# A twentieth early weight load for the expert layer, and scatters and gathers at other places between its steps

## The reference, cut to what matters

```python
def expert_choice_ffn(x, w_router, w_gate_up, w_down):
    B, T, D = x.shape                                  # 1, 512, 1024
    cap = EC_CAPACITY_FACTOR * T // N_EXPERTS          # 64 tokens for each of 16 experts
    logits = jnp.einsum('btd,de->bte', x, w_router)
    aff = jax.nn.softmax(logits, axis=-1)
    gate, idx = lax.top_k(jnp.swapaxes(aff, 1, 2), cap)
    xs = x[bidx, idx]                                  # each expert gathers its 64 tokens
    h = jnp.einsum('becd,edf->becf', xs, w_gate_up)    # 1024 -> 2 x 1024
    hg, hu = jnp.split(h, 2, axis=-1)
    ye = jnp.einsum('becf,efd->becd', jax.nn.silu(hg) * hu, w_down)   # 1024 -> 1024
    ye = ye * gate[..., None]
    return jnp.zeros_like(x).at[bidx, idx].add(ye)     # scattered back, summed
```

## Time and profile before

| what | value |
|---|---|
| median of 3 runs | 2118.4 us (2118.39 to 2119.78) |
| the profiled execution: its time, its span | 2120.5 us, 2118.7 us |
| busy in the span: TensorE, VectorE, ScalarE, GpSimd | 98%, 48%, 35%, 7% |
| TensorE's granted clock, mean | 0.997 |
| moved by DMA | 352 MB, 166 GB/s on average |
| the expert steps, first up step to the end | 1661.7 to 2118.7 us |

### The profile page before, as it was taken

How to read it: one execution, slowest core, us unless ns; L and a number is a source line. 1 busy time by engine, 2 the same in 40 slices (tenths; PEclk the granted TensorE clock), 3 DMA queues, 4 the chain that set the end, 5 groups by cost and what they waited for, 6 DMA issues and landing times.

```text
span 2118.7 us, 24857 instructions
## 1 busy us (share of the span) xinstructions
PE 2086.6 (98%) x10137; PEld 1517.1 (72%) x10137; DVE 1023.1 (48%) x1515; ACT 750.2 (35%) x1076; POOL 146.4 (7%) x149
## 2 busy tenths in 40 slices
PE   9999999999999999999999999999999999999998
PEld 7878888888777778888888877777787544444433
DVE  7875433445666664434446656564464312122123
ACT  7774322323455543222334456533333100011012
POOL 0220000001000020000001010062101000000000
PEclk9999999999999999999999999999999999999999
DMA  6233223324211123233233322242236999999996
GB/s 218 75 104 110 83 83 124 100 69 121 70 60 59 61 92 105 69 123 99 82 88 119 115 60 77 60 89 72 73 110 231 401 426 412 427 427 426 426 427 275
DMA packets 88944, 352.09 MB, mean 166 GB/s; under 512 B 9472, under 2 KB 24064, under 8 KB 64512
## 3 DMA queue, kind: packets, MB, share of 16 engines
q1 hardware_dynamic: 83856, 342.48, 43.6%
q0 software_dynamic: 2192, 2.63, 1.0%
q10 hardware_dynamic: 2784, 5.41, 0.7%
HBM read 347.06 MB, written 2.10 MB: 165 GB/s over the span
## 4 chain that ended last, share of the span: by engine, by line
PE 86%; DVE 5%; DMA 4%; ACT 3%; issue 2%; POOL 0%; ACTq 0%; DVEq 0%; SPq 0%; POOLq 0%
PE PS L2184 20%; PE PS L2185 19%; PE PS L2186 19%; PE PS L2591 9%; PE PS L2631 4%; DMA SL<-in_wgu_dram 3%; PE PS L2227 2%; DMA SL<-in_wdn_dram 1%; DVE WL L1664 1%; PE PS L2301 1%; PE PS L2575 1%; PE PS L2325 1%; PE PS L2315 1%; PE PS L2576 1%; DVE XC L1731 1%
## 5 line engine op out<-in xcount | busy, mean ns | idle before, releaser
L2184 PE MATMUL PS<-HH,WH 128*128 128x512 f32 x1392 | 553.9, 398 | 3.0 <-DVE HL L1704 2.2
L2186 PE MATMUL PS<-HH,WL 128*128 128x512 f32 x1392 | 543.0, 390 | 0.0
L2185 PE MATMUL PS<-HL,WH 128*128 128x512 f32 x1392 | 542.6, 390 | 0.0
L1664 DVE TENSOR_TENSOR WL<-RAW,WH 128x1024 fp32r<-128x1024 f32 (+4 forms) x302 | 343.5, 1138 | 294.6 <-ACT WH L1340 293.7
L1340 ACT ACTIVATE WH<-RAW 128x1024 fp32r<-128x1024 f32 (+4 forms) x302 | 286.5, 951 | 308.5 <-PE PS L2186 278.3
L2184 PEld LDWEIGHTS PS<-HH,WH 128*128 128x128 f32 x1392 | 261.7, 188 | 69.1 <-issue 10.3
L2186 PEld LDWEIGHTS PS<-HH,WL 128*128 128x128 f32 x1392 | 261.7, 188 | 55.6
L2185 PEld LDWEIGHTS PS<-HL,WH 128*128 128x128 f32 x1392 | 262.0, 188 | 52.9 <-issue 1.0
L2591 PE MATMUL PS<-SL,XS 128*64 128x512 f32 x928 | 220.8, 595 | 6.4 <-DMA SL<-in_wgu_dram 5.8
L2591 PEld LDWEIGHTS PS<-SL,XS 128*64 128x64 f32 x928 | 70.4, 137 | 135.7 <-issue 133.7
L2186 PE MATMUL PS<-MH,WL 128*128 128x512 f32 x352 | 136.9, 389 | 0.0
(11 more groups left out here) (375 smaller groups left out, 2740.5 us busy)
## 6 DMA issues: line engine op xcount, KB each, us to landing
SL<-in_wgu_dram SPq DMA_DIRECT2D x116, 1024.0 KB, 21.8
SL<-in_wdn_dram SPq DMA_DIRECT2D x55, 1024.0 KB, 24.8
RAW<-in_w_dram SPq DMA_DIRECT2D x46, 512.0 KB, 3.4
RAW<-in_wg_dram SPq DMA_DIRECT2D x44, 512.0 KB, 3.4
RAW<-in_wu_dram SPq DMA_DIRECT2D x44, 512.0 KB, 3.4
RAW<-in_wd_dram SPq DMA_DIRECT2D x32, 384.0 KB, 3.1
RAW<-in_wqkv_dram SPq DMA_DIRECT2D x24, 512.0 KB, 3.5
RAW<-in_wd_dram SPq DMA_DIRECT2D x32, 320.0 KB, 2.9
```

The costliest lines, as they stand in the source:

```text
L1664: e.tensor_tensor(wl, raw, wh.bitcast(F), ALU.subtract).then_inc(*wlo.did("u", u))
L2184: e.matmul(out, wh[:, w], xh, start=k == 0, stop=False)
L2185: e.matmul(out, wh[:, w], xl, start=False, stop=False)
L2186: m = e.matmul(out, wl[:, w], xh, start=False, stop=k == g.total - 1)
```

## The change

It has four parts. (1) A twentieth slot, used once, for load 15: the gate half goes to the storage of GT, the two quarters of the up half to HG[0] and HG[1], by three transfers with one semaphore; the matmuls now address each slot as four pieces of 512 columns. This takes load 15's place in the ring from it, and the loads behind it move by one slot until load 41. (2) The gathers of q + 1 keep only their first two in the odd pair, behind up step 1; the other six move into the even pair, two behind up steps 1, 3 and 5, just ahead of the steps that read them, as in pair 0 before. (3) In pairs 1 to 6 the scatter moves from in front of the turns to behind the down steps: block 0 behind step 0, block 1 behind step 1, blocks 2 and 3 behind step 2. (4) In pairs 2, 4 and 6 the one-hot's transposes and the next one-hot move from behind down step 0 to behind down step 3.

```diff
--- before.py
+++ after.py
@@ -30,7 +30,7 @@
 CAP = 64
 NEARLY = 10
 NRING = 16
-SPARE = ((4, 23), (0, 39), (1, 39))
+SPARE = ((4, 23), (0, 39), (1, 39), (15, 15))
 NBACK = 4
 NGATE = 5
 NWARM = 21
@@ -843,12 +843,12 @@
             gather(0, 1)
         for k in range(8):
             o.add("up", i, k)
-            if i % 2 and i < 7 and k % 2:
-                gather(q + 1, k - 1)
-                gather(q + 1, k)
-            if i == 0 and k % 2 and k < 7:
-                gather(0, k + 1)
-                gather(0, k + 2)
+            if i % 2 and i < 7 and k == 1:
+                gather(q + 1, 0)
+                gather(q + 1, 1)
+            if i % 2 == 0 and k % 2 and k < 7:
+                gather(q, k + 1)
+                gather(q, k + 2)
             if i == 7 and 1 <= k < 5:
                 scatter(6, k - 1)
                 o.add("halves", k - 1)
@@ -864,8 +864,6 @@
             o.release(("h", i, 2 + n), "mul", i, n)
         if i == 0:
             o.add("alpha")
-        elif i < 7:
-            scatter(i - 1, *range(4))
         for half in range(2):
             o.claim("ht", i, half)
             o.add("h_turn", i, half)
@@ -884,13 +882,15 @@
             break
         for k in range(4):
             o.add("down", i, k)
-            if i % 2 == 0 and k == 0:
+            if i % 2 == 0 and k == (3 if i else 0):
                 for j in range(2):
                     o.claim("gt", "e", q, j)
                     o.add("scatter_t", q, j)
                     o.release(("gt", "e", q, j), "turn", "gt", q, j)
                 if q < 3:
                     o.add("one_hot", q + 1)
+            if 0 < i < 7 and k < 3:
+                scatter(i - 1, *((0,), (1,), (2, 3))[k])
         y_out(0)
         y_out(1)
 
@@ -1109,8 +1109,12 @@
         pa.close()
         YOH = sb("YOH", [128, D], R, px)
         YOL = sb("YOL", [128, D], R, px)
+        pa = ExitStack()
+        SG = sb("SG", [128, 2 * T], F, pa)
+        pa.close()
         GT = [sb(f"GT{i}", [128, T], R, px) for i in range(2)]
-        SL = early + late + once + x_slots
+        SL = [[t[:, 512 * n:512 * n + 512] for n in range(4)] for t in early + late + once + x_slots]
+        SL.append([SG[:, 0:512], SG[:, 512:1024], HG[0], HG[1]])
         assert CST["ones"] + 2560 == NCST and len(early) == NEARLY and len(SL) == NRING + len(SPARE)
         BN = sb("BN", [128, 4, 2, 6], F, px)
         MV = sb("MV", [128, 4, 2], F, px)
@@ -1199,6 +1203,8 @@
         ring = [i for i in range(len(SL)) if i not in where]
         where.update((i, j) for j, i in enumerate(ring))
         issue = ring[:NEARLY] + [SPARE[0][0]] + ring[NEARLY:NEARLY + 2] + [SPARE[1][0], SPARE[2][0]] + ring[NEARLY + 2:]
+        issue.append(SPARE[3][0])
+        whole = early + late + once + x_slots
         turns = [where[i] for i in range(len(SL))]
         for i in range(len(SL), len(loads)):
             while i > spare.get(turns[0], i):
@@ -1242,10 +1248,14 @@
                 if j in last_in:
                     e.wait_ge(*ex("w", last_in[j] // 2))
                 last_in[j] = i
-                if i < len(loads) - 4:
-                    e.dma_start(SL[j][:, :], src).then_inc(*d_slot[j].did(i))
+                if i == SPARE[3][0]:
+                    e.dma_start(SG[:, :], src[:, 0:1024]).then_inc(*d_slot[j].did(i, "gates"))
+                    e.dma_start(HG[0], src[:, 1024:1536]).then_inc(*d_slot[j].did(i, "first ups"))
+                    e.dma_start(HG[1], src[:, 1536:2048]).then_inc(*d_slot[j].did(i))
+                elif i < len(loads) - 4:
+                    e.dma_start(whole[j][:, :], src).then_inc(*d_slot[j].did(i))
                 else:
-                    dst = SL[j][:, :].rearrange("p (e f n) -> p e f n", e=2, f=2)
+                    dst = whole[j][:, :].rearrange("p (e f n) -> p e f n", e=2, f=2)
                     e.dma_start(dst[:, 0], src[0]).then_inc(*d_slot[j].did(i, "first"))
                     e.dma_start(dst[:, 1], src[1]).then_inc(*d_slot[j].did(i))
             for half, c in ((0, 2), (0, 0), (0, 6), (0, 4), (1, 2), (1, 6)):
@@ -2589,7 +2599,7 @@
                         for e2 in range(2):
                             x0 = (2 * (i % 2) + e2) * 64
                             m = e.matmul(bank("h", i, n)[64 * e2:64 * e2 + 64, :], XS[:, k, x0:x0 + 64],
-                                         SL[slot(l0 + e2)][:, 512 * n:512 * n + 512], start=k == 0, stop=k == 7)
+                                         SL[slot(l0 + e2)][n], start=k == 0, stop=k == 7)
                         if k == 7 and n == 2:
                             m.then_inc(*ex.did("h", i, 0))
                     m.then_inc(*ex.did("w", 12 * i + k))
@@ -2629,7 +2639,7 @@
                         for n in range(2):
                             for e2 in range(2):
                                 m = e.matmul(bank("y", i, n)[64 * e2:64 * e2 + 64, :], HT[k // 2][:, 2 * (k % 2) + f, 64 * e2:64 * e2 + 64],
-                                             SL[slot(l0 + e2)][:, 1024 * f + 512 * n:1024 * f + 512 * n + 512],
+                                             SL[slot(l0 + e2)][2 * f + n],
                                              start=k + f == 0, stop=k == 3 and f == 1)
                     m.then_inc(*ex.did("w", 12 * i + 8 + k))
                     if k == 3:
@@ -2641,9 +2651,8 @@
                     e.wait_ge(*d_slot[slot(l0)](l0))
                     for f in range(2):
                         for e2 in range(2):
-                            col = 1024 * e2 + 512 * f
                             m = e.matmul(bank("y", 7, n)[64 * e2:64 * e2 + 64, :], HT[1][:, 2 * x + f, 64 * e2:64 * e2 + 64],
-                                         SL[slot(l0)][:, col:col + 512], start=False, stop=x + f == 2)
+                                         SL[slot(l0)][2 * e2 + f], start=False, stop=x + f == 2)
                     if x:
                         m.then_inc(*ex.did("y", 7, n))
                 elif kind == "scatter":
```

## The result

The changed kernel takes 2124.0 us (median of 9 runs, 2122.7 to 2126.8), the kernel before 2118.7 beside it (9 runs, 2118.4 to 2120.7). The ratio is 1.0025 with a 95% interval of 1.0016 to 1.0033: 5.2 us slower. I had forecast 2116.2 and a range up to 2119.0. The profiled execution took 2123.2 us with a span of 2121.4; it reached its first up step 1.4 us earlier than the one of before (1660.27 against 1661.66), so of its experts the loss is 4.1 us.

The account below looks back on a forecast made before the run. The weight stream was taken as the bound: the end is load 187's landing plus 31.5 us. Early load -0.4, second gap -1.8, order on TensorE 0 give -2.2 us from 2118.4: 2116.2 us, range 2113.5 to 2119.0.

Parts of the forecast that it names:

- 0 (order on TensorE): Term of the sum for the moved gathers and scatters: TensorE's work is only reordered, costing 0 us.
- Rival (4): TensorE becomes the bound in pair 6, gather pairs holding up the next up steps: +4.3 us, 2122.7; chance 0.05.
- The early load: Load 15 in its own storage: worth 2.46 us until about 1680, 0 to 1.5 after 1705; taken as 0.4.
- 34 slots: Loads allowed before any down step ends: 34 instead of 35, so load 34 waits for down step (0,0), 1702.12.
- the first gap: Weight stream at 172 GB/s from 1663 to 1668 us, 2.98 us lost; the change was to fill 2.46.
- a new loss before 1706: New gap in the weight stream at load 34: 0.9 us on the lagging engine, 2.4 on most.
- Rival (1): Early load kept whole, no new gap at load 34: 4.2 to 4.7 us gained, 2113.7 to 2114.2; chance 0.12.
- The second gap: Weight stream at 236 GB/s from 1757 to 1761 us; down step (1,0) starting earlier closes it, gaining 1.78 us.
- my two bounds of 0.8 and 2.2: Limits in us on the gain from closing the second gap, if a few of the 16 engines lag by 1.4.
- Rival (3): Each piece of split load 15 pays the fixed time, two more at 2.3 us: +0.3, 2118.7; chance 0.08.

Follow-up runs that it names:

- g1: Kernel before with, in pair 4 alone, the scatter in three blocks behind down steps 0, 1 and 2 and its one-hot behind step 3: 2118.8 us, ratio 0.9998.
- A: The changed kernel, with all four parts of the change: 2124.0 us against 2118.7 for the kernel before beside it.
- e1: Changed kernel with the scatter back in one block in front of the turns, early load and moved gathers kept: 2118.9 us, ratio 0.9998 to before.
- e4: Changed kernel with a pair's whole scatter in one block behind down step 0 instead of three blocks: 2119.9 us, ratio 1.0004 to before.
- B: The kernel before the change: 2118.7 us beside the changed kernel, 2118.6 to 2119.3 beside the experiments.
- f2: Kernel before with the moved gathers and later one-hot alone, 19 early loads, scatter in front of the turns: 2118.3 us, ratio 0.9996.
- e2: Changed kernel with the gathers back in the odd pairs, in four blocks of two: 2126.1 us, ratio 1.0032 to before.
- f3: Changed kernel without its early load (19 slots, no split), order of steps kept: 2123.7 us, ratio 1.0021 to before.
- f4: Changed kernel with the scatter back in front of the turns in pair 4 alone: 2118.7 us, ratio 0.9999 to before.
- e3: Kernel before with the twentieth early load alone, order of steps as before: 2119.7 us, ratio 1.0002.
- f1: e1's kernel with load 23 taking load 4's slot again and load 24 load 3's: 2117.1 us, ratio 0.9993 to before.
- g2: Changed kernel with scatter blocks 0 and 1 in front of the turns, 2 and 3 in one block behind down step 0: 2118.8 us, ratio 0.9997 to before.

## Why the prediction was wrong

**The step that failed** is "The work is moved, not removed, so TensorE gains nothing in total", and with it "0 (order on TensorE)" in the sum. I had TensorE start pair 6 4 us earlier than before, at 1985.7. It started at 1992.7, and the 1.4 us by which this execution reached its first up step earlier have to be added to that: 8.4 us later than I counted. The work that TensorE really does, pair by pair (first row of the table against the second, pair 6 of before taken at 48.6, which g1 shows without waits): 55.1 + 48.6 + 55.1 + 62.1 + 55.1 + 48.6 = 324.6 before, 50.6 + 56.4 + 50.7 + 72.3 + 50.7 + 56.4 = 337.1 after, **12.5 us more**. Where it comes from:

- The scatter's place (A against e1): 1.9 us in each odd pair, 1.1 in pair 2 and in pair 6 (that pair by its like, since e1 waits there), 4.4 in pair 4, 12.3 in all. Of it 0.76 a pair is three blocks instead of one (e4), and 0.3 a pair is one block behind a down step instead of in front of the turns (pair 2 of e4 against e1). Neither stood in my sum. The rest of an odd pair is the bare wait for the product, 0.8 a time, which I had counted.
- Pair 4: 1.5 us idle in front of the turns, where VectorE and ScalarE have the evictions of L2150 and L1649 ahead of the product, and 1.7 us for the stretch at 1.2 GHz. I had looked for cover in the odd pairs only. In before, the scatter in front of the turns was busy work in just this time.
- The gathers (e1 against B, f2): 6.4 us less in an odd pair, 6.8 more in pair 2 (and in pair 6 by its like) and 5.9 in pair 4. Together 0.3 more, so that half of the step was right.

Against 12.5 stands what TensorE had to spare: 53.9 - 48.6 = 5.3 us of waits in pair 6 and 75.4 - 72.3 = 3.1 in pair 7, together 8.4. I had 4 for pair 7, nearly right, and used it for nothing, since I saw no lateness. **12.5 - 8.4 = 4.1 us** is the loss of the profiled execution; that much is bookkeeping, since both numbers come from these same traces. TensorE's list of waits names only 6.5 of the 8.4 us, 4.4 in pair 6 and 2.1 in pair 7. The test is whether the 8.4 hold elsewhere. The same sum for the kernels in which TensorE is late or nearly late (added work of pairs 1 to 6 from the table, less 8.4, never under 0) stands beside the medians:

| kernel | added | less 8.4 | measured by medians |
|---|---|---|---|
| A | 12.5 | 4.1 | 5.2 |
| e2 | 14.6 | 6.2 | 6.8 |
| f3 | 14.0 | 5.6 | 5.1 |
| e4 | 9.0 | 0.6 | 0.6 |
| f4 | 8.1 | 0 | 0.1 |
| g1 | 5.6 | 0 | -0.2 |

One spare sum of 8.4 us comes within 1.1 us of six kernels, though not in order: A and f3 change places. How long the clock is low in pair 4 differs from one execution to another (3.4 us in A and e2, 6.8 in e4, f3 and g1, half of which is lost). The five slower of A's nine runs have a mean granted clock of 0.996 and the four faster, the profiled one among them, 0.997; a longer fall in the slower ones fits A's remaining 1.1 us but is not shown, since these means don't say where in the run the clock was low.

**Rival (4)** named the right bound and gave 2122.7, with a chance of 0.05. Its mechanism, gather pairs holding up steps in pair 6, did not happen: no wait for XS is in any list. The right bound for another reason is no credit to it.

**The early load.** 34 slots, the issue of load 34 at 1700.7 (1702.1 - 1.4) and the first gap nearly filled came as predicted, and so did a new loss before 1706. I took 0.4 us of gain; e3 shows 0.4 of loss, within the bounds of the medians and below my own 0 to 1.5. It fills 2.2 us and gives 3.6 back up to 1756. What I missed is that most of the head start is gone before load 34 is reached: 2.3 us at load 24, 0.1 at load 27, nothing at load 33 (A in the table under f2). Loads 25 to 33 are issued at the same times after the first up step as before, within 0.3 us, because they wait for their slots, and the slots come free at TensorE's pace. SyncE's waits in A from 1666.6 to 1712 us show it:

```profile
SPq L1256 <- PE PS L2601: 25.3, 7, 4.9
SPq L1256 <- PE PS L2641: 12.0, 3, 5.6
```

One load more in front did not bring the later issues forward. When loads 25 and 27 were issued, two loads were under way instead of three, and they landed 3.8 and 3.2 us behind the load before them instead of 2.44. I had let the stream run at full rate until load 34. Rival (1), the load kept whole, falls with this.

**The second gap** closed, with down step (1,0) starting at 1744.11 against 1745.5 - 1.4 predicted. In the landings of f2 it is worth 0.9 us at load 187 and 2.3 at load 153, about my two bounds of 0.8 and 2.2; I took 1.8 between them. That a load lands with the slowest of the engines, from which I had these bounds, fits the late landings, but no row shows the engines one by one. The stream had in any case no say in A, since nothing on TensorE waited for it.

**The split** costs little if anything: the last piece of load 15 lands 2.94 us behind load 19 in A and 2.50 in e3, where whole loads follow one another in 2.44. Rival (3) stays with no support; of DMA: Bandwidth & Descriptors in the Trainium skill, Rules for kernel authors (1 MiB or more in one DMA), which I had set against the split, this case shows no effect beyond the 0.4 us of e3, where three transfers stand for one.

## What to carry to other kernels

An engine whose waits near the end add up to a few microseconds is all but the bound. Estimate its spare time from how long its last stages take with the waits and without, and count every edit of its order against it, edits together and not one by one: here 8.4 us were to spare and 12.5 were spent. The list of waits alone gave 6.5, too little. A block of matmuls in front of a step that needs another engine's result is cover; before it is moved, look up in every pair, in the other engines' own order, what it covers. A load that is started earlier gains nothing later if the loads behind it wait for slots that the engine frees at its own pace. And what a gap in a stream is worth should be read at several loads, since the last landing of one execution can be off by one late load, 1.4 us here.

## What the runs showed of the hardware

- A block of scatter matmuls among down steps costs time at its borders. Its first matmul takes 0.43 us and the next ones 0.23 (chain of A), and three blocks instead of one cost 0.76 us a pair, whether the pair is odd or even (e4). In front of the turns and behind gathers, as in the kernel before, the first one takes 0.23.
- The granted clock fell from 2.4 to 1.2 GHz in pair 4 of A, and a down step took 4.83 us instead of 3.58. TensorE had been idle for 1.0 us, did a turn, was idle for 1.5 us more, and did small matmuls for 1.9 us before the fall. The same two idle stretches stood in pair 4 of e2, e4, f3 and g1, and the clock fell there too: in e4 and g1 still within the second, in f3 0.8 us and in e2 2.2 us behind it. In the seven kernels whose scatter lay in front of pair 4's turns, whole or half (before, e1, e3, f1, f2, f4, g2), only the idle 1.0 us was there, and the clock stayed up.
- With four or more loads under way when a load was issued, it landed 2.44 to 2.45 us behind the one before it (medians of the twelve kernels). With only two the median was 2.96 us in A (six loads) and 2.46 in B (four loads). A few loads of an execution landed up to 1.7 us later than that; those of B, f1 and f2 named under f2 came shortly behind a 16 KB instruction packet.
